# Modulation products of a two-block transformer kernel moved to other places of TensorE's order; one modulation sum kept in rows of x

## The reference, cut to what matters

```
mod_l = silu_c @ w_mod[l] + b_mod[l]      # first block: shift, scale, gate, for x
mod_c = silu_cc @ w_mod[l] + b_mod[l]     # and the same for ctx
...
ada = (cond_act @ w_ada + b_ada)[:, None, :]         # second block, each layer
sh1, sc1, g1, sh2, sc2, g2 = jnp.split(ada, 6, axis=-1)
u = layer_norm(x) * (1 + sc1) + sh1
...                                                  # projections, branches, gates
x = layer_norm(ALPHA * x + g1 * mixed) * ln1_g + ln1_b
u2 = layer_norm(x) * (1 + sc2) + sh2
hdn = jnp.square(jax.nn.relu(u2 @ w_up + b_up))
x = layer_norm(ALPHA * x + g2 * (hdn @ w_down)) * ln2_g + ln2_b
```

## Time and profile before

| | us |
|---|---|
| median of 3 runs | 1468.96 |
| lowest and highest | 1465.49 and 1472.9 |
| the profiled execution, its own time | 1472.11 |
| its span, first to last instruction | 1470.3 |

### The profile page before, as it was taken

How to read it: one execution, slowest core, us unless ns; L and a number is a source line. 1 busy time by engine, 2 the same in 40 slices (tenths; PEclk the granted TensorE clock), 3 DMA queues, 4 the chain that set the end, 5 groups by cost and what they waited for, 6 DMA issues and landing times.

```text
span 1470.3 us, 18937 instructions
## 1 busy us (share of the span) xinstructions
PE 1358.4 (92%) x7889; PEld 1104.4 (75%) x7889; DVE 954.0 (65%) x1227; ACT 497.0 (34%) x742; POOL 144.5 (10%) x163
## 2 busy tenths in 40 slices
PE   5999999999997899999997999997999999799996
PEld 1588755535784548989985988885988898698895
DVE  3666475856648775676677766656765767755546
ACT  1422025402335313543232333432354332243431
POOL 2010110101000010011331000001000232100000
PEclk9999999999999999999997999998999999799998
DMA  9452351324430067564765676653665685355551
GB/s 343 144 174 90 131 179 51 115 91 138 172 129 1 30 229 250 187 239 167 258 234 188 228 253 218 221 179 117 217 215 212 216 296 192 113 197 176 192 179 57
DMA packets 104918, 257.97 MB, mean 175 GB/s; under 512 B 8217, under 2 KB 11770, under 8 KB 104578
## 3 DMA queue, kind: packets, MB, share of 16 engines
q1 hardware_dynamic: 80554, 171.78, 34.3%
q0 software_dynamic: 20192, 75.58, 14.3%
q10 hardware_dynamic: 4088, 9.41, 1.9%
HBM read 255.70 MB, written 1.05 MB: 175 GB/s over the span
## 4 chain that ended last, share of the span: by engine, by line
PE 76%; DVE 15%; ACT 4%; issue 3%; DMA 2%; POOL 1%; ACTq 0%; SPq 0%; POOLq 0%; DVEq 0%
PE bank L734 73%; PE bank L880 3%; DVE weights_low L2026 2%; ACT weights_high L1444 1%; DVE modulation_sums L1844 1%; DMA x<-in_ctx_dram 1%; ACT odd_prob L1619 1%; POOL inverse_roots L647 1%; DMA weight_ring<-in_w_in_dram 1%; DVE statistics L1986 1%; DVE even_A L1971 1%; DVE statistics L1884 1%; DVE x L2459 1%; DVE dulation_sums_of_context L1844 0%; DVE x L1985 0%
## 5 line engine op out<-in xcount | busy, mean ns | idle before, releaser
L2026 DVE TENSOR_TENSOR weights_low<-weight_ring,weights_high 128x2048 fp32r<-128x2048 f32 (+1 forms) x124 | 276.9, 2235 | 278.4 <-ACT weights_high L1444 278.4
L1444 ACT ACTIVATE weights_high<-weight_ring 128x2048 fp32r<-128x2048 f32 (+1 forms) x124 | 231.2, 1865 | 465.4 <-PE bank L734 407.5
L734 PE MATMUL bank<-uT_high,weights_high 128*128 128x256 f32 (+1 forms) x1200 | 347.0, 289 | 4.8 <-DVE uT_low L2302 2.8
L734 PE MATMUL bank<-uT_low,weights_high 128*128 128x256 f32 (+1 forms) x1200 | 344.9, 287 | 0.0
L734 PE MATMUL bank<-uT_high,weights_low 128*128 128x256 f32 (+1 forms) x1200 | 344.5, 287 | 0.0
L734 PEld LDWEIGHTS bank<-uT_high,weights_high 128*128 128x128 f32 (+1 forms) x1200 | 234.2, 195 | 9.3 <-issue 6.5
L734 PEld LDWEIGHTS bank<-uT_low,weights_high 128*128 128x128 f32 (+1 forms) x1200 | 234.5, 195 | 1.0
L734 PEld LDWEIGHTS bank<-uT_high,weights_low 128*128 128x128 f32 (+1 forms) x1200 | 234.2, 195 | 0.5
L1844 DVE SCALAR_TENSOR_TENSOR modulation_sums<-modulation_ring,silu_c_columns,modulation_sums 128x1024 f32<-128x1024 f32 x128 | 175.3, 1369 | 14.2 <-DMA modulation_ring<-in_w_ada_dram 10.9
L734 PE MATMUL bank<-weights_high,hidden_high 128*128 128x512 f32 x256 | 101.8, 397 | 6.1 <-DVE weights_low L2026 6.1
L734 PE MATMUL bank<-weights_low,hidden_high 128*128 128x512 f32 x256 | 101.2, 395 | 0.0
(11 more groups left out here) (292 smaller groups left out, 2188.9 us busy)
## 6 DMA issues: line engine op xcount, KB each, us to landing
weight_ring<-in_w_in_dram SPq DMA_DIRECT2D x52, 1024.0 KB, 6.8
modulation_ring<-in_w_ada_dram POOLq DMA_DIRECT2D x48, 1024.0 KB, 7.3
weight_ring<-in_w_up_dram SPq DMA_DIRECT2D x32, 1024.0 KB, 5.4
weight_ring<-in_w_down_dram SPq DMA_DIRECT2D x32, 1024.0 KB, 4.9
modulation_ring<-in_w_mod_dram POOLq DMA_DIRECT2D x16, 1024.0 KB, 5.4
weight_ring<-in_o_w_in_dram SPq DMA_DIRECT2D x10, 1024.0 KB, 5.4
weight_ring<-in_w_branch_dram SPq DMA_DIRECT2D x16, 512.0 KB, 3.7
weight_ring<-in_w_o_dram SPq DMA_DIRECT2D x8, 1024.0 KB, 7.0
```

Of the source, the lines that this page charges most:

```text
L734: return track(pe.matmul(*args, **kw))
L1444: act.activation(ring[:, s, 0:kn * cols], wring[:, slot, 0:kn * cols], ACT.Copy).then_inc(S["high_ready"], 1)
L2026: dve.tensor_tensor(lo[:, s, 0:kn * cols], wring[:, slot, 0:kn * cols], hi[:, s, 0:kn * cols].bitcast(F32), ALU.subtract).then_inc(w_free[ ...
```

## The change

The sums are computed as before, from the same chunks in the same order. What moves:
- Part 2: after Fourier steps g = 0 (stream x) and g = 2 (stream ctx), in bank 7; VectorE copies its columns out after `f2` of group 1.
- Part 4: stream x at the start of head step h = 8, stream ctx after the last head step, in banks 0 and 1 in turn.
- Part 5: after the first scores of the odd attention, ahead of part 6, in banks 4 and 5. Part 6's sum is cleared after its first two chunks are asked for, and VectorE multiplies part 6 after the rotary angles.
- In a layer: parts 1 and 2 after `o1`, ahead of the turned tiles; part 3 (g2) between the two turned tiles, with its sum in x[:, 2, :], so that its `mod_start` waits for no reduction; part 4 at j = 8, beside part 5. VectorE copies parts 1 and 2 out ahead of the second tile's normalisation.

```
+        def sums(sec, c, v=0):
+            if sec.layer is not None and c == 3:
+                return x[:, TC, :]
+            return acc[v][:, c % 2, :]
@@ mod_start
-                if sec.layer is not None or c >= PE_MODS + 2:
+                if (c != 3) if sec.layer is not None else c >= PE_MODS + 2:
                     pool.wait_ge(S["acc_used"], sec.at("acc_used", c - 1))
...
@@ GpSimd, first section
-            mod_part(sec, 6)
+            mod_chunks(sec, 6, 0, 1)
+            mod_start(sec, 6)
+            mod_chunks(sec, 6, 2, 3)
@@ GpSimd, a layer that is not the last, after the merges
-                    mod_start(sec, 4)
                     mod_chunks(sec, 4, 0, 1)
                     tile_roots(1)
+                    mod_start(sec, 4)
                     mod_chunks(sec, 4, 2, 3)
@@ TensorE, first section
-            reduce_part(2)
             tokens_out(both("qa"), [("qa", i) for i in range(TALL)], h_e_tokens, QR)
...
+                if g in (0, 2):
+                    reduce_part(2, g // 2)
                 if g > 0:
                     copied(("f1", g - 1, 0))
...
+                if h == MH:
+                    reduce_part(4, 0)
                 if 1 <= h <= MH:
...
-                if h == 3:
-                    reduce_part(4)
+            reduce_part(4, 1)
...
             tokens_out(both("eout0"), [("eout", 0, i) for i in range(TALL)], eyT_tokens, COLS)
-            reduce_part(5)
...
                 if p == 0:
+                    reduce_part(5)
                     reduce_part(6)
@@ TensorE, a layer
-                    if g in MODS_BESIDE:
-                        reduce_part(MODS_BESIDE.index(g))
+                    if g == 1:
+                        reduce_part(0)
                 tokens_out(both("o0"), [("o", 0, i) for i in range(TC)], ui, COLS, wait=u_split(1))
                 tokens_out_by_tile(both("o1"), [("o", 1, i) for i in range(TC)], ui)
-                reduce_part(3)
-                turn_xn("x2T", TC)
+                reduce_part(1)
+                reduce_part(2)
+                turn_xn("x2T", TC, between=lambda: reduce_part(3))
...
                     if j == 8 and not sec.last:
+                        reduce_part(4)
                         reduce_part(5)
...
-                    if j == 6 and not sec.last:
-                        reduce_part(4)
@@ ScalarE: gate_rows(4, ...) and gate_rows(5, ...) follow these places
@@ VectorE
-            mod_columns(2, mcol, 0)
             low_e("kva", 0)
...
+                if g == 1:
+                    mod_columns(2, mcol, 0)
...
-            for q in range(4):
-                gemv(6, q)
             dve.wait_ge(pos_in, 16)
...
+            for q in range(4):
+                gemv(6, q)
             for v in range(2):
                 copied(("mod", 4, v, 1))
...
-                residual("o", 1, "norm1")
+                def columns_of_mlp():
+                    mod_columns(1, mcol2, 0)
+                    mod_columns(2, mcol2, 1)
+                residual("o", 1, "norm1", columns_of_mlp)
```

More of the change, by code:

```diff
@@ L126, in first_jobs @@
             jobs += [(("S", h, i), (0, 1, 7)) for i in range(3)]
+        if h >= MH:
+            jobs += [(("mod", 4, h - MH, i), (0, 1)) for i in range(2)]
         if 1 <= h <= MH:
@@ L130, in first_jobs @@
             jobs += [(("PV", (h - 2) // 2), (5, 6))]
-        if h == 3:
-            jobs += mod_jobs(FIRST_MODS, 4, last)
-    jobs += [(("eout", 0, t), lo) for t in range(TALL)] + mod_jobs(FIRST_MODS, 5, last)
+    jobs += [(("eout", 0, t), lo) for t in range(TALL)]
     jobs += [(("eout", 1, t), lo) for t in range(TALL)]
@@ L179, in layer_jobs @@
             jobs += [(("down", t, h), (4 + 2 * t + h,)) for t in range(TC) for h in range(2)]
-        if j in (6, 8) and not last:
-            jobs += mod_jobs(LAYER_MODS, j // 2 + 1, lo)
+        if j == 8 and not last:
+            jobs += mod_jobs(LAYER_MODS, 4, lo) + mod_jobs(LAYER_MODS, 5, lo)
     return jobs
-MODS_BESIDE = (1, 4, 6)
 CHUNKS_BESIDE = (2, 2, 2, 2, 2, 2, 2)
@@ L812, in reduce_part @@
                 pe.wait_ge(m_free[slot], before + 1)
-                if rows:
-                    for v in range(streams):
+                for v in parts or range(streams):
+                    if rows:
                         for h in range(2):
                             o = start(("mod", c, v, h))
-                            ins = product(o[:, :], ones, acc[v][:, c % 2, COLS * h:COLS * h + COLS],
+                            ins = product(o[:, :], ones, sums(sec, c, v)[:, COLS * h:COLS * h + COLS],
                                             start=True, stop=True)
                             done(ins, ("mod", c, v, h))
-                else:
-                    o = start(("mod", c))
-                    for v in range(streams):
+                    else:
+                        o = start(("mod", c)) if v == 0 else bank[sec.bank(("mod", c), 0)[0]]
                         for k in range(KD):
-                            ins = product(o[:, v * KD + k:v * KD + k + 1], acc[v][:, c % 2, P * k:P * k + P],
+                            ins = product(o[:, v * KD + k:v * KD + k + 1], sums(sec, c, v)[:, P * k:P * k + P],
                                             ones[:, 0:1], start=True, stop=True)
-                    done(ins, ("mod", c))
-                signal(ins, S["acc_used"])
+                        if v == streams - 1:
+                            done(ins, ("mod", c))
+                    if v == streams - 1:
+                        signal(ins, S["acc_used"])
             def features_out(names, jobs, src, ntok, per, width=P, wait=lambda k: None):
@@ L1476, in tanh_tile, with gate_rows @@
                 act.activation(dst, o[:, :], ACT.Tanh, scale=0.5).then_inc(S["tanh_done"], 1)
-            def gate_rows(c, dst, scale=1.0):
-                _, streams, _ = sec.mods[c]
-                for v in range(streams):
+            def gate_rows(c, dst, scale=1.0, parts=(0,)):
+                for v in parts:
                     for h in range(2):
@@ L2503, in _ @@
                         low(f"up{j + 1}" if j < 7 else "down7")
-                    if j == 6 and not sec.last:
-                        mod_columns(4, mcol, 0)
                 if not sec.last:
+                    mod_columns(4, mcol, 0)
                     mod_columns(5, mcol, 1)
```

37 lines of the change are left out of this document (20 added, 17 removed).

## The result

| | before | after |
|---|---|---|
| median of the runs, us | 1470.93 (4) | 1450.84 (4) |
| lowest to highest | 1465.49 to 1473.87 | 1445.25 to 1452.23 |
| profiled execution, own time | 1472.11 | 1452.23 |
| its span | 1470.3 | 1450.4 |
| mean granted clock in it | 0.962 | 0.967 |

The ratio of the runs is 0.9854, 95% interval 0.9826 to 0.9881. The forecast was 1448, with a range of 1440 to 1460; the measured time lies inside it, 3 us above the forecast.

What follows compares the result with a forecast made beforehand. TensorE, holding 76% of the chain of waits, was taken as the bound. Terms of 6.15 + 6.4 - 1.5 + 2.4 - 2.2 + 5.9 + 3.0 + 1.2 make 21.3 us off 1469.0, giving 1447.7, said 1448; range 1440 to 1460.

Steps and rivals of the forecast that it cites:

- Part 2: Between fgate and qa: removing exposed records gives 4.20 us plus 2.25 of clock, less 0.3 for copies; gain 6.15.
- Part 4: Even attention: scores of h = 4 start 6.4 us earlier; first pair's new place free, second pair costs 1.5.
- Part 5: Between the even output projections, gain 2.4 us; at its new place in the odd attention, cost 2.2.
- The layers' parts 1 and 2: Ends of gate tiles 4 and 6: four places give 1.47 us each, 5.9 in all, plus 3.0 of clock.
- the first rival: Gate tiles and MLP steps are bound by ScalarE and VectorE splitting weights, so layer moves give nothing: 1458 us; 8%.
- The clock as a whole: Whole kernel: 5.25 of the 21.3 us predicted gain is granted clock returned behind removed reductions.
- the third rival: More clock returns in the Fourier stage, odd head and layer ends, three or four stretches of 1.5 us: 1442; 14%.
- the second rival: Clock isn't returned, because it falls elsewhere as often: gain 16.1 us, time 1453; 22%.
- Part 4 of the layer: MLP, one layer: leaving j = 6 saves 1.7 us, joining j = 8 costs 0.5 beyond a wait; gain 1.2.
- Parts 3 and 4 of a layer, their clearing at 0: In a layer: g2's clearing no longer waits for TensorE, chunks are asked for as before; cost 0.
- The floor: Skill page's start-to-start floor of about 25 ns per product: 32 records take 0.8 us, time 1458; given 1%.
- the slower one: Part 6's clearing waits for the last gate rows, VectorE empties output tiles late and TensorE stands: 1476 or more; 2%.

Runs made afterwards that it cites:

- part2_back: The changed kernel with part 2's 32 one-column records put back between the products of fgate and qa; median 1455.85 us.
- layer_parts_back: The changed kernel with parts 1 and 2 of each hybrid layer reduced behind gate tiles 4 and 6 again, by one-column products; median 1459.89 us.
- layer_parts_wide: The changed kernel with parts 1 and 2 of each layer back behind gate tiles 4 and 6, each by two 512-column products; median 1456.05 us.
- cols_behind_maxima: The changed kernel with VectorE copying part 6's columns behind the first maxima of the odd attention, not ahead of them; median 1447.82 us.

## Why the prediction was right

- *Part 4* was the largest term and right in mechanism: the scores of h = 4 follow the products of h = 3 straight. By the starts it is 6.7 and not 6.4; 0.3 I can't place. The first new pair was free, and gave 0.5 besides; the second cost 1.5 as worked out (2.24 in a wait of 1.41, and ScalarE's last copy).
- *Part 2*: records exposed at the old place, hidden at the new one, as said. Mis-sized was the clock: 2.25 counted in full, and 0.7 more of it inside the 4.20 taken for records, where of two profiles with the records at the old place only one shows it. How much it is in the mean the runs leave open, from nothing to all of it.
- *The layers' parts 1 and 2*: 1.47, 1.46, 1.44 and 1.47 against 1.47 each. Their clock is 3.0 in the two profiles, as counted, and 3.7 to 4.5 by the mean clock of the runs that put them back.
- *Dense stretches that stay dense*: not quite. The prediction called it a sign of being wrong if TensorE stood idle for more than 0.6 us at a tile's end. It does so once, 1.17 us behind gate tile 5 of layer 0, where the chain goes through the transfer of weights (11.56 us) and ScalarE; so 0.6 of the 1.5 that the clock gives back there is lost. In all eight profiles with the new order at these tiles that wait is 0.69 to 1.57 us, and behind the other tiles 0.54 to 0.62. It is the first rival in small: where TensorE already waits for the weights, less work for it gives nothing.
- *The clock as a whole*: 5.25 counted and 4.8 estimated from the runs is in part luck. In the two profiles part 2 and the layers give about 6, the end of layer 1 gives 2.2 that the sum didn't have (the third rival named the layer ends), and the step at j = 8, gate tile 3 of layer 0, the last MLP steps and the start take 1.2, 1.4, 1.5 and 1.8 that it didn't have either (the second rival).
- *Part 5*: the wait without it is 1.05 where 1.4 was assumed, so the gap shrank by 2.7 and the start moved by 2.6; the new place cost 1.7 to 1.8 where 2.2 was taken, since two wide products start 1.77 apart from what follows at full clock.
- *Part 4 of the layer*: the step that failed. "1.7 - 0.5 = 1.2" held for the work (1.2 in the profiles), and 1.2 of clock went against it; the prediction looked for clock given back where products left, and not for clock taken where sixteen records became 32.
- *Parts 3 and 4 of a layer, their clearing at 0*: the clearing of part 4's sum moved from beside VectorE's cast to beside its normalisation, in layer 0. That gives 0.9 and costs 0.6; the prediction looked at what a clearing waits for and not at what runs beside it, and the 0 came out near 0.3 by luck.
- *The floor*: in part2_back 32 records take 3.49 us at full clock (97.16 to 100.65), 109 ns each, not the 25 of the Trainium skill's page "TensorE: Matmul & The Clock Gate", section "Wait — 56ns, not 53.3ns?"; here each record has a full load of weights, and the measurement decides.
- *The idle gaps* of the same page of the Trainium skill, section "HAM oscillation — how this bites in real kernels": layer_parts_back and layer_parts_wide differ in clock with TensorE busy in both, so gaps aren't what cost it at these places. The second rival, that it wouldn't be returned, is out for the gate tiles; that the clock falls elsewhere instead is right for the places named above, and the mean clock still rises from 0.9635 to 0.9674.
- Of the rivals, the slower one began as described: VectorE reaches the first output tile 19.2 us after the projections' start (304.34 - 285.18) where it was 17.5. It came to nothing: by the third tile VectorE waits for TensorE again (0.90 us).

## What to carry over

Price a short reduction by what stands next to it: in a dense stretch it costs its whole length, and one-column products can cost as much again in clock behind them. Put it where TensorE already waits, keep such runs short and apart (32 records in a row were followed by half clock in 20 of 22 places outside the layers' ends, sixteen at j = 8 in none of four), and let no consumer's queue read its result ahead of the work that the chain needs. When a stretch gives way, look whether a transfer or another engine takes over the chain there. Where the clock differs from run to run, compare times at one clock too: here it cut the scatter within a kernel from 3.2 to 1.4 us. But don't read single microseconds from it between kernels, and add up the undone steps: here they sum to more than the whole.

## What the runs showed of the hardware

- TensorE can lose half its clock while it is busy all the time: 0.68 and 0.63 behind sixteen one-column records, 1.00 behind four wide ones in the same place. Behind part 3's 32 one-column records it does so in all twelve profiles (0.51 in after).
- The 24 us at the end of layer 1 have a mean clock of 0.64 in before and 0.86 in after; 17.1 us at half clock in both profiles with the old order, 6.8 to 10.2 in all ten with the new.
- A VectorE operation of 128x1024 took 0.80 to 0.81 us alone and 1.41 beside GpSimd's clearing of another 128x1024 tile, in all ten profiles that have them together. A cast of 128x512 took 2.40 us with such a clearing beside its end and 1.51 without, in the same place.
- Executions of one kernel differ in mean clock by up to 0.011 (cols_behind_maxima: 0.959 to 0.970), which is 13 us by the fit; over the 106 runs it accounts for 83% of the variance within kernels.
